# Gate matrix stored by group of experts, and early activations loaded a trip ahead into four buffers

## The chip, the cores and the metric

One core of one Trainium2 chip. The metric is the time of one execution on the device in microseconds (us), the median of several runs. The kernel before ran three times: 4664.34, 4643.26 and 4653.38 us, median 4653.38.

## The reference, cut to what matters

One layer for 640 tokens (8 x 16 of running streams, 512 of a new one), width 2048: a joint projection, two attentions, a gated merge, LayerNorm, and then the expert layer (PEER) which the change touches. Each token picks, for each of 8 heads, 16 of 128 x 128 single-neuron experts, and sums their outputs.

```python
experts = e1 * PEER_KEYS + e2
gate = jax.nn.softmax(sc, axis=-1)
u = jnp.take(u_table, experts, axis=0)
act = jax.nn.gelu(jnp.einsum('nhkd,nd->nhk', u, xt), approximate=False)
w = (gate * act).astype(xt.dtype)
v = jnp.take(v_table, experts, axis=0)
return jnp.einsum('nhk,nhkd->nd', w, v)
```

## The kernel before, in words

**Two ways through the expert layer.** For 256 of the 640 tokens (two blocks of 128) the expert rows are gathered: GpSimd issues an indirect transfer of 128 rows (1 MB) for each of 128 picks, for two tables and two blocks (`gather`, L379), and VectorE takes each of these 512 steps in one pass of 2048 columns (`gather_step`, L1414; L1420 for u rows, L1423 for v rows). Four row buffers rotate. For the other 384 tokens (N2) the layer is dense: all 16384 experts are computed by TensorE, and a gate matrix that is zero for experts not picked selects among them.

**Units.** TensorE's work is cut into units of 1 MB of weights (128 x 2048 f32), streamed by SyncE into two buffers. ScalarE copies a half into the high part (`split_high`, L1021, copy at L1024), GpSimd subtracts for the low part (`low`, L352, L356), and TensorE does three products (high x high, high x low, low x high), 48 matmuls of 384 columns a unit. A group is 4 x 128 experts: four activation units (L639) and four output units (`out_units`, L698, matmul at L703). There are 32 groups. Output units leave partial sums in four PSUM banks, and VectorE adds each into the result (`add_out`, L1436, L1443); a matmul into a bank waits for that add.

**The gate matrix.** Before the late part, a loop of 6 trips (L1001 to L1014) builds it, 64 tokens a trip: VectorE makes one-hot rows (L1403, L1404), TensorE multiplies them (L691) beside the units of the early activations, ScalarE empties the banks into one of two buffers of 2 MB (L1007), and after every 8th of the 96 steps stores one as a block of 32 tokens into the DRAM tensor `gate_matrix` (`G_s`, L134), 16 KB in a row per partition (L1011). `early_activation` (L975) in steps 8 and 15 of each trip stores a 192 KB activation (L980): the activations of the first 4 groups (16 units) are made here, as no gates exist yet. At the end ScalarE waits for the stores (L1018) before it copies the first late weights, and GpSimd does so as well (L441).

**The late part.** Its order is written out. First `EARLY` = 4 trips (L1096) of 12 units: four activation units of group 4+i, its four output units, and four output units of early group i. Then 24 plain groups of 8 units. For each group ScalarE loads that group's gates for all 384 tokens into `G4` (`load_gates`, L1026): per partition 12 pieces (one per block of 32 tokens) of 4 x 32 values, 512 bytes. VectorE multiplies activations by gates (`product`, L1426, L1429), ScalarE copies the high part of the products (`high_part`, L1031, L1033), VectorE makes the low part (`low_part`, L1431, L1433). For an early group the activations come back from DRAM into `act_t` (L190), two buffers, by `load_act` (L1035): the first two are issued behind the trip's first gate load, and the last two when the low parts of the first two are done, both within the trip. VectorE waits for each in `early_product` (L1526).

```python
                for e in range(2):
                    load_act(i, q, e, 8 * i + 2)
                for v in range(2):
                    out_unit(2 * i, first + EG, v, k + EG + v)
                for e in range(2):
                    high_part(q, e, 1, act_t[e])
                out_unit(2 * i, first + EG, 2, k + EG + 2)
                for e in range(2, 4):
                    load_act(i, q, e, 8 * i + 7 + e - 2)
```

**What orders the rest.** The gather steps are dealt over the positions (units) of the late part by a table of room per unit (`ROOM`, `deal`, `STEPS`). GpSimd runs per unit two subtractions and, between them, the gathers dealt to it (`position`, L416); VectorE runs its steps between products and adds; ScalarE's queue holds copies, gelu, the gate loads and the activation loads in program order. All transfers share 16 transfer engines.

## Time and profile before

| | |
|---|---|
| median of 3 runs | 4653.38 us (4643.26 to 4664.34) |
| the profiled execution's own time | 4646.84 us |
| its span | 4645.1 us |
| TensorE matmuls busy | 4319.6 us (93%) |
| VectorE / GpSimd / ScalarE busy | 2683.9 / 2586.4 / 1060.3 us |
| transfers | 1082.02 MB, 233 GB/s over the span |
| gate store / gate load / early activation load, issue to landing (median) | 6.3 / 15.6 / 10.9 us |

The durations of the sections below are from the profiled execution, one run whose own time is 4646.84 us; it lies 6.5 us under the median. "Busy" counts an engine's instructions, not its waits; a transfer share of 1.0 means that all 16 engines had packets under way the whole time (packets of different queues can overlap a little, so the share can pass 1).

### The profile page before, as it was taken

What the parts mean: (1) busy time and instruction counts of PE and PEld (TensorE: products, weight loads), DVE (VectorE), ACT (ScalarE), POOL (GpSimd) and SP (SyncE); (2) the same over time, 40 slices, a digit from 0 to 9 for tenths busy, and PEclk for the clock granted to TensorE, in tenths of its full rate; (3) what the DMA queues carried; (4) which work ended last, traced back from release to release, by engine and by line L of the source; (5) the groups of instructions that cost most, each with busy time, mean ns of one, the idle gap of its engine ahead of it and who ended that gap; (6) DMA issues with size and microseconds to landing.
All of it is one profiled execution on the core that took longest, in us unless ns stands there. A gap on an engine that the chain in (4) does not pass through costs nothing.

```text
span 4645.1 us, 71896 instructions
## 1 busy us (share of the span) xinstructions
PE 4319.6 (93%) x26508; PEld 4144.1 (89%) x26508; DVE 2683.9 (58%) x4808; ACT 1060.3 (23%) x1861; POOL 2586.4 (56%) x1653
## 2 busy tenths in 40 slices
PE   8999999999989997985888999999999999999997
PEld 8999888878889996985878999999999999999996
DVE  1000233344442314898896777777777777777776
ACT  1000122222221102101223222222223222223223
POOL 4455322222235453443335777877777878777783
PEclk9999999999999999997999999999999999999998
DMA  5222322322233221111447999999999999999994
GB/s 199 99 100 95 118 109 102 111 88 78 78 136 121 100 95 54 63 63 56 172 158 287 362 366 366 399 398 402 398 392 377 396 387 406 394 396 400 386 411 199
DMA packets 265977, 1082.02 MB, mean 233 GB/s; under 512 B 24496, under 2 KB 89136, under 8 KB 181168
## 3 DMA queue, kind: packets, MB, share of 16 engines
q0 software_dynamic: 74736, 544.24, 28.7%
q1 hardware_dynamic: 87840, 388.01, 22.6%
q10 hardware_dynamic: 103328, 148.96, 9.4%
q8 instruction: 25, 0.41, 0.0%
q14 instruction: 48, 0.39, 0.0%
HBM read 1019.65 MB, written 66.85 MB: 234 GB/s over the span
## 4 chain that ended last, share of the span: by engine, by line
PE 60%; DVE 12%; POOL 10%; DMA 8%; issue 7%; ACT 1%; ACTq 0%; DVEq 0%; POOLq 0%
PE banks L461 29%; PE banks L703 12%; PE banks L639 11%; POOL w_lo L356 7%; POOL work L384 2%; DMA work<-in_v_rows,idx_all 2%; DMA work<-in_u_rows,idx_all 2%; PE banks L530 2%; PE banks L492 1%; PE banks L691 1%; DMA work<-early_act 1%; DVE work L1404 1%; DMA rows_own<-in_v_rows,idx_all 1%; PE banks L500 1%; DVE mv_hi L1403 1%
## 5 line engine op out<-in xcount | busy, mean ns | idle before, releaser
L356 POOL TENSOR_TENSOR w_lo<-w_raw,w_hi 128x1024 fp32r<-128x1024 f32 x480 | 1154.6, 2406 | 414.2 <-ACT w_hi L1024 409.7
L362 POOL TENSOR_SCALAR w_hi<-w_raw 128x2048 fp32r<-128x2048 f32 x130 | 253.1, 1947 | 1475.7 <-PE banks L461 1269.0
L461 PE MATMUL banks<-mv_hi,w_hi 128*128 128x256 f32 x3648 | 863.5, 318 | 62.1 <-DVE mv_lo L1150 37.5
L461 PE MATMUL banks<-mv_lo,w_hi 128*128 128x256 f32 x3648 | 836.2, 311 | 0.0
L461 PE MATMUL banks<-mv_hi,w_lo 128*128 128x256 f32 x3648 | 835.1, 310 | 0.0
L703 PE MATMUL banks<-mv_hi,w_hi 128*128 128x384 f32 x2048 | 704.2, 344 | 92.9 <-DVE work L1443 82.7
L461 PEld LDWEIGHTS banks<-mv_hi,w_hi 128*128 128x128 f32 x3648 | 652.3, 189 | 125.9 <-issue 102.5
L1024 ACT ACTIVATE w_hi<-w_raw 128x1024 fp32r<-128x1024 f32 x480 | 507.5, 1060 | 998.6 <-PE banks L703 741.8
L639 PE MATMUL banks<-mv_hi,w_hi 128*128 128x384 f32 x2048 | 695.8, 340 | 15.2 <-POOL w_lo L356 11.5
L703 PE MATMUL banks<-mv_hi,w_lo 128*128 128x384 f32 x2048 | 697.2, 340 | 0.0
L703 PE MATMUL banks<-mv_lo,w_hi 128*128 128x384 f32 x2048 | 697.2, 340 | 0.0
L366 POOL TENSOR_TENSOR w_lo<-w_raw,w_hi 128x512 fp32r<-128x512 f32 x520 | 681.9, 1343 | 10.8
L639 PE MATMUL banks<-mv_lo,w_hi 128*128 128x384 f32 x2048 | 687.2, 336 | 0.0
L639 PE MATMUL banks<-mv_hi,w_lo 128*128 128x384 f32 x2048 | 687.0, 335 | 0.0
L461 PEld LDWEIGHTS banks<-mv_lo,w_hi 128*128 128x128 f32 x3648 | 669.7, 189 | 0.0
L461 PEld LDWEIGHTS banks<-mv_hi,w_lo 128*128 128x128 f32 x3648 | 669.1, 189 | 0.0
L1423 DVE SCALAR_TENSOR_TENSOR banks<-work,subkt,banks 128x2048 f32<-128x2048 f32 x192 | 451.6, 2352 | 102.3 <-DMA work<-in_v_rows,idx_all 101.8
L1420 DVE CUSTOM_DVE_ANT_0 work<-work,banks 128x2048 f32<-128x2048 f32 x192 | 438.0, 2283 | 106.0 <-DMA work<-in_u_rows,idx_all 103.7
L703 PEld LDWEIGHTS banks<-mv_hi,w_hi 128*128 128x128 f32 x2048 | 394.7, 193 | 110.7 <-DVE work L1443 94.9
L639 PEld LDWEIGHTS banks<-mv_hi,w_hi 128*128 128x128 f32 x2048 | 387.2, 189 | 16.0 <-issue 11.7
L703 PEld LDWEIGHTS banks<-mv_lo,w_hi 128*128 128x128 f32 x2048 | 394.8, 193 | 0.0
L703 PEld LDWEIGHTS banks<-mv_hi,w_lo 128*128 128x128 f32 x2048 | 394.1, 192 | 0.0
(155 smaller groups left out, 4788.2 us busy)
## 6 DMA issues: line engine op xcount, KB each, us to landing
w_raw<-in_wstream SPq DMA_DIRECT2D x480, 512.0 KB, 7.9
w_raw<-in_wstream SPq DMA_DIRECT2D x130, 1024.0 KB, 4.8
gate_matrix<-work ACTq DMA_DIRECT2D x12, 2048.0 KB, 6.3
work<-gate_matrix ACTq DMA_DIRECT2D x32, 768.0 KB, 15.6
out_p<-work ACTq DMA_DIRECT2D x34, 320.0 KB, 2.2
work<-out_p ACTq DMA_DIRECT2D x34, 320.0 KB, 3.4
gate_scratch<-work ACTq DMA_DIRECT2D x32, 320.0 KB, 2.2
work<-gate_scratch ACTq DMA_DIRECT2D x16, 640.0 KB, 3.9
```

The source lines that it names most:

```text
L356: pool.tensor_tensor(w_lo[s][:, part], raw[s][:, part], w_hi[s][:, part].bitcast(f32), ALU.subtract) \
L362: pool.tensor_scalar(w_hi[s][:, :], raw[s][:, :], 1.0, 0.0, ALU.mult, ALU.add).then_inc(hi_done, 1)
L366: last = pool.tensor_tensor(w_lo[s][:, part], raw[s][:, part], w_hi[s][:, part].bitcast(f32), ALU.subtract)
L384: pool.indirect_dma_start(rows_t[n % ROWS], None, (u_rows, v_rows)[pick // PICKS % 2], bass.IndirectOffsetOnAxis(ap=idx_all[:, pick:pick + ...
L461: last = pe.matmul(acc(dst, h), a[s][:, P * k:P * k + P], b[h][:, k, :], start=(k == k_first and n == 0), stop=(k == k_last and n == 2))
L492: last = pe.matmul(bank[:, 0:w], q_t[rows, end - P:end], k_t[rows, end - w:end], start=True, stop=True)
L530: last = pe.matmul(o, v_nat[:, P * kb + HD * hh:P * kb + HD * hh + HD], pt[:, P * c:P * c + P], start=(c == 0), stop=(c == nk - 1))
L639: last = pe.matmul(banks[:, bank, 0:N2], a[s][:, P * k:P * k + P], b[1][:, k, :], start=(k == 0 and n == 0), stop=(k == KT_N - 1 and n == 2))
L703: last = pe.matmul(banks[:, d, 0:N2], a[v % 2][:, at:at + P], b[z][:, e, :], start=(e == 0 and n == 0), stop=(e == EG - 1 and n == 2))
L1024: act.activation(w_hi[s][:, HALVES[h]], raw[s][:, HALVES[h]], ACT.Copy).then_inc(hi_late, 1)
L1420: ins = dve.tensor_tensor_reduce(rows, rows, nat, 1.0, 0.0, ALU.mult, ALU.add, act_n[:, pick % PICKS:pick % PICKS + 1])
L1423: ins = dve.scalar_tensor_tensor(nat, rows, act_n[:, pick % PICKS:pick % PICKS + 1], nat, ALU.mult, ALU.add)
```

## The change

The DRAM tensor of the gate matrix is laid out as (group, partition, block, expert, token) in place of (block, partition, expert, token). A gate load is then one row of 6 KB per partition; a gate store writes, for each partition, 32 pieces of 512 bytes, one per group. `act_t` has four buffers in place of two (the two new ones lie in columns 2304 to 3071 of the same work area, free in the late part until the last sums), with a semaphore each, and the four activations of an early group are loaded together: for trip 0 right behind the very first gate load, for trip i+1 at the end of trip i's first set of output units, behind the gate load that stands there. In the trip itself nothing is loaded but gates.

```diff
@@ -131,7 +131,7 @@
         bs_a = dram("bias_sample_a", (16, P, 144))
         a_s = dram("early_act", (N_EARLY, P, N2))
         hb_s = dram("block_h", (P, D))
-        G_s = dram("gate_matrix", (GBLK, P, KEYS, GT))
+        G_s = dram("gate_matrix", (GROUPS, P, GBLK, EG, GT))
 
         raw = [sb(f"w_raw{s}", [P, D]) for s in range(2)]
         w_hi = [sb(f"w_hi{s}", [P, D], f32r) for s in range(2)]
@@ -187,7 +187,7 @@
         psum = W2[:, 2688:2688 + N2]
         mean_t, rstd_t = W2[:, 0:T], W2[:, T:2 * T]
         sq_t = x_res
-        act_t = [W2[:, N2 * s:N2 * s + N2] for s in range(2)]
+        act_t = [W2[:, N2 * s:N2 * s + N2] for s in (0, 1, 6, 7)]
         pick_t = [W2[:, N2 * (q + 2):N2 * (q + 3)] for q in range(3)]
         oh1 = W2[:, 5 * N2:5 * N2 + 8 * P].rearrange("p (n e) -> p n e", n=8)
         G4 = W2[:, 2 * N2:6 * N2].rearrange("p (b e t) -> p b e t", b=GBLK, e=EG)
@@ -283,7 +283,7 @@
 
         oh_ready, g_full, g_evac = sem("oh_ready"), sem("g_full"), sem("g_evac")
         act_stored = [sem(f"act_stored{s}") for s in range(2)]
-        act_in = [sem(f"act_in{s}") for s in range(2)]
+        act_in = [sem(f"act_in{e}") for e in range(EG)]
 
         rows_in = [sem(f"rows_in{s}") for s in range(ROWS)]
         idx_ready, acc_high, rows_used, nat_ready, act_n_ready, act_n_gelu = (
@@ -1008,8 +1008,8 @@
                                    banks[:, 2 + q % 2, :].rearrange("p (t e) -> p e t", t=4), ACT.Copy).then_inc(g_evac, 1)
                     if qq == 7:
                         act.wait_ge(g_evac, 16 * i + q + 3)
-                        act.dma_start(G_s[ds(2 * i + w, 1)].rearrange("a p e t -> p (a e t)"),
-                                      g_buf[w].rearrange("p e t -> p (e t)")).then_inc(g_stored[w], 16)
+                        act.dma_start(G_s[:, :, ds(2 * i + w, 1), :, :].rearrange("g p a e t -> p g (a e t)"),
+                                      g_buf[w].rearrange("p (g e) t -> p g (e t)", e=EG)).then_inc(g_stored[w], 16)
                     if q in (8, 15):
                         early_activation(TAIL + 2 * i + q // 15, q // 15, TAIL // 2 + i)
 
@@ -1025,17 +1025,17 @@
 
             def load_gates(g, q):
                 act.wait_ge(w_prod, 1 + 4 * q)
-                act.dma_start(G4.rearrange("p b e t -> p b (e t)"),
-                              G_s[:, :, ds(EG * g, EG), :].rearrange("b p e t -> p b (e t)")).then_inc(g4_in, 16)
+                act.dma_start(G4.rearrange("p b e t -> p (b e t)"),
+                              G_s[g].rearrange("p b e t -> p (b e t)")).then_inc(g4_in, 16)
 
             def high_part(q, e, z, src):
                 act.wait_ge(w_prod, 1 + 4 * q + e + 1)
                 act.activation(ww_hi[z][:, e, :], src, ACT.Copy).then_inc(wwh_done, 1)
 
-            def load_act(g, q, e, after):
-                act.wait_ge(w_ready, after)
-                act.dma_start(act_t[e % 2], a_s[ds(EG * g + e, 1)].rearrange("a p t -> p (a t)")) \
-                    .then_inc(act_in[e % 2], 16)
+            def load_acts(i):
+                act.wait_ge(w_ready, 8 * i + 2)
+                for e in range(EG):
+                    act.dma_start(act_t[e], a_s[EG * i + e]).then_inc(act_in[e], 16)
 
             def act_units(g, q, first):
                 for e in range(EG):
@@ -1093,24 +1093,20 @@
                     split_high(v % 2, (first - U_LATE) // 2 + 1 + v // 2, 1)
 
             load_gates(EARLY, 0)
+            load_acts(0)
             for i in range(EARLY):
                 first, q, k = U_LATE + 12 * i, 2 * i + 1, 12 * i
                 for e in range(EG):
                     act_unit(EARLY + i, 2 * i, first, e, k + e)
                 load_gates(i, q)
-                for e in range(2):
-                    load_act(i, q, e, 8 * i + 2)
-                for v in range(2):
+                for v in range(EG):
+                    if v >= 2:
+                        for e in (2 * v - 4, 2 * v - 3):
+                            high_part(q, e, 1, act_t[e])
                     out_unit(2 * i, first + EG, v, k + EG + v)
-                for e in range(2):
-                    high_part(q, e, 1, act_t[e])
-                out_unit(2 * i, first + EG, 2, k + EG + 2)
-                for e in range(2, 4):
-                    load_act(i, q, e, 8 * i + 7 + e - 2)
-                for e in range(2, 4):
-                    high_part(q, e, 1, act_t[e % 2])
-                out_unit(2 * i, first + EG, 3, k + EG + 3)
                 load_gates(EARLY + i + 1, q + 1)
+                if i + 1 < EARLY:
+                    load_acts(i + 1)
                 for v in range(EG):
                     out_unit(q, first + 2 * EG, v, k + 2 * EG + v)
             for g in range(2 * EARLY, GROUPS):
@@ -1524,8 +1520,8 @@
                         steps(k + e + 1, 1)
 
             def early_product(i, e):
-                dve.wait_ge(act_in[e % 2], 16 * (2 * i + e // 2 + 1))
-                product(act_t[e % 2], e)
+                dve.wait_ge(act_in[e], 16 * i + 16)
+                product(act_t[e], e)
 
             for i in range(EARLY):
                 q, first, k = 2 * i + 1, U_LATE + 12 * i + EG, 12 * i
@@ -1540,7 +1536,7 @@
                             early_product(i, e)
                     if v >= 2:
                         for e in (0, 1) if v == 2 else (2, 3):
-                            low_part(q, e, 1, act_t[e % 2])
+                            low_part(q, e, 1, act_t[e])
                     add_out(2 * i, v, first, parts=range(2))
                     if v > 1:
                         steps(k + EG + v, 1)
```

## Rows read from the trace of the kernel before

**Rows 1.** The page: busy time of each engine, and the transfer share in 40 slices.
```profile
PE 4319.6 (93%) x26508; PEld 4144.1 (89%) x26508; DVE 2683.9 (58%) x4808; ACT 1060.3 (23%) x1861; POOL 2586.4 (56%) x1653
...
DMA  5222322322233221111447999999999999999994
```

**Rows 2.** Windows by stage: length, busy PE, PEld, DVE, ACT, POOL, clock, share, GB/s.
```profile
2240.00:2460.00 220.00, 178.78 (x1218) 171.91 (x1216) 216.90 (x698) 57.68 (x100) 65.03 (x47) 0.97 0.41 160
2460.00:2900.00 440.00, 399.29 (x2203) 395.05 (x2204) 312.56 (x371) 125.61 (x147) 320.50 (x187) 0.95 0.93 354
2900.00:3400.00 500.00, 485.55 (x2749) 482.03 (x2748) 380.66 (x338) 145.44 (x172) 396.38 (x243) 0.99 1.01 399
```

**Rows 3.** Windows: one trip, one group, and behind one stall.
```profile
2544.30:2657.20 112.90, 103.19 (x576) 101.92 (x576) 82.39 (x99) 30.51 (x37) 81.78 (x50) 0.97 0.95 365
...
3734.00:3804.20 70.20, 68.16 (x384) 67.84 (x384) 50.22 (x59) 20.26 (x24) 54.07 (x33) 0.98 0.99 384
...
2545.00:2560.00 15.00, 15.00 (x78) 15.00 (x77) 13.53 (x15) 2.92 (x4) 11.92 (x8) 0.86 0.87 297
```

**Rows 4.** Chain of waits, 3040 to 3110 us.
```profile
3059.07 33.28 PE banks L639 x192
```

**Rows 5.** TensorE's timeline at its stalls; idle time and its releaser in brackets.
```profile
2544.32 0.69 PE L703 MATMUL banks<-mv_hi,w_hi 128*128 128x384 f32 x1 [5.34 <-DVE work L1443]
...
2768.83 0.69 PE L703 MATMUL banks<-mv_hi,w_hi 128*128 128x384 f32 x1 [5.18 <-DVE work L1443]
...
2881.79 0.69 PE L703 MATMUL banks<-mv_hi,w_hi 128*128 128x384 f32 x1 [5.73 <-DVE work L1443]
...
2962.28 0.44 PE L703 MATMUL banks<-mv_hi,w_hi 128*128 128x384 f32 x1 [2.00 <-DVE work L1443]
...
3734.02 0.69 PE L703 MATMUL banks<-mv_hi,w_hi 128*128 128x384 f32 x1 [3.82 <-DVE work L1443]
```

**Rows 6.** VectorE's timeline, 2533 to 2545 us.
```profile
2533.37 0.08 DVE L1420 DVE_READ_ACCUMULATOR2_ANT subkt<- 128x1 f32 x1
2538.76 0.56 DVE L1429 TENSOR_TENSOR work<-work 128x384 f32<-128x384 f32 x1 [5.30 <-DMA work<-early_act]
2542.09 0.56 DVE L1429 TENSOR_TENSOR work<-work 128x384 f32<-128x384 f32 x1 [2.77 <-DMA work<-early_act]
...
2543.72 1.01 DVE L1443 TENSOR_TENSOR work<-work,banks 128x384 f32<-128x384 f32 x2
```

**Rows 7.** ScalarE's timeline, 2504 to 2531 us (ACTq: issues of transfers).
```profile
2504.16 5.51 ACTq L1037 DMA_DIRECT2D work<-early_act  x1
...
2513.57 2.01 ACT L1024 ACTIVATE w_hi<-w_raw 128x1024 fp32r<-128x1024 f32 x2 [7.75 <-issue]
...
2530.70 0.90 ACTq L1037 DMA_DIRECT2D work<-early_act  x2
```

**Rows 8.** Queues (packets, MB, share): rows 3663.3-3734, gate loads 4000-4600, one store 2254-2262.
```profile
q0 software_dynamic: 2576, 18.73, 64.8%
...
q10 hardware_dynamic: 12416, 6.29, 3.7%
...
q10 hardware_dynamic: 128, 2.10, 61.9%
```

**Rows 9.** ScalarE's timeline at the end of the gate matrix.
```profile
2456.99 0.34 ACTq L1011 DMA_DIRECT2D gate_matrix<-work  x1
...
2458.17 0.34 ACTq L980 DMA_DIRECT2D early_act<-work  x1
2464.04 1.06 ACT L1024 ACTIVATE w_hi<-w_raw 128x1024 fp32r<-128x1024 f32 x1 [6.04 <-DMA early_act<-work]
```

**Rows 10.** ScalarE's timeline around a gate store in the build stage.
```profile
2256.63 0.34 ACTq L1011 DMA_DIRECT2D gate_matrix<-work  x1
...
2259.86 0.60 ACT L1007 ACTIVATE work<-banks 128x512 f32<-128x512 f32 x1 [2.21 <-PE banks L691]
2264.63 0.60 ACT L1007 ACTIVATE work<-banks 128x512 f32<-128x512 f32 x1 [4.17 <-PE banks L691]
```

## Prediction

> **What bounds the kernel now.** I read the page's busy shares first: TensorE is busy for 93% of the span, and in the page's slices the share of the transfer engines is 9 from slice 22 on [rows 1]. So the kernel falls into a part where only TensorE is full and a part where the transfers are full as well. The windows by stage say which wait counts where [rows 2]. While the gate matrix is built (2240 to 2460 us) VectorE is busy for 216.9 of 220 us and the transfer engines for 41%: VectorE sets that stage. In the four early trips (2460 to 2900) TensorE is busy for 399 of 440 us and the transfers for 93%. In the plain groups behind them TensorE has 97% and the transfers 1.01, 399 GB/s.
>
> Cut into one trip (12 units) and one group (8 units) the balance is plain [rows 3]: a trip lasts 112.9 us with TensorE busy for 103.2 and a transfer share of 0.95; a group lasts 70.2 us with 68.2 and 0.99. The chain of waits has a stretch with 192 matmuls in 33.28 us, 173.3 ns each [rows 4]. A trip's 576 matmuls would take 99.8 us at that, a group's 384 66.6 us. The rest is what can be won.
>
> TensorE's timeline shows where the rest sits [rows 5]. In each of the four early trips (three of the stalls stand there) TensorE waits 5.2 to 5.7 us for VectorE's add at L1443, always at the same place, and restarts with a 0.69 us matmul. In the 24 plain groups the common stall is about 2 us (3.82 in the longest). Behind the stall at 2544 the granted clock is 0.86 over 15 us [rows 3], a part of them at 1.2 instead of 2.4 GHz: 78 matmuls ran where 15 / 0.1733 = 87 fit, 1.5 us lost.
>
> Why VectorE is late there is in its own timeline [rows 6]: from 2533.4 it waits 5.30 us for an early activation, then 2.77 us for the next, and only at 2543.72 does it come to the adds that TensorE stands for. ScalarE issued these two loads at 2530.70, since their buffers were those of the first two activations; they had landed for it 8.1 and 11.4 us later, behind weights and rows [rows 7]. The same view shows a second thing: the first two loads, issued right behind the gates' 1536 pieces of 512 bytes, hold ScalarE for 5.51 us and then until 2513.57, where its next copy of weights could begin.
>
> **The change part by part.**
> *Four activation buffers.* This removes the 5.30 + 2.77 us from VectorE. Its chain products, high copies, low parts, adds then starts at 2533.4 and needs, as at 2538.8 to 2543.7 without the second wait, about 2.2 us; a copy by ScalarE lies between. The adds come at about 2535.6 to 2536, 3 us before TensorE arrives (2544.32 - 5.34 = 2538.98). So the whole 5.3 us goes, and with it the 1.5 us of slow clock: 112.9 - 6.8 = 106.1 us per trip. What is late next is the transfers: 0.95 x 112.9 = 107.3 us of engine time per trip, less 2 x 0.8 for the gates (below), 105.7 us. Both sides say 106: 7 us per trip, **-28 us** over four. Ends: -32 (8 per trip, transfers at a share just above 1) and -14, if half comes back in another wait.
>
> *Where the loads go now.* Four loads of 192 KB are issued in a row behind the trip's last gate load, a trip ahead; for trip 0 at 2464 in place of nothing. On ScalarE that is four issues of some 0.4 us where the next one is not held. They stand ahead of the next weight copy, which GpSimd's subtraction and then its row gathers wait for. The work that hides the 1.6 us is the other unit's matmuls, 48 x 173 ns = 8.3 us; without that cover it would be up to 6 us over four trips. The load waits for the last low part of its trip, which comes 1.2 us after the product that the gate load waits for. At 2464 TensorE needs its first product only after a unit of matmuls. I cost both at 0.
>
> *Gates read as 6 KB pieces.* A 512-byte piece costs one engine 0.037 x 16 x 600 / 12416 = 28.6 ns, so a gate load holds each engine for 96 x 28.6 = 2.75 us. 6 KB pieces are not in this trace; the nearest are the 8 KB pieces of the rows, 25.5 bytes per ns with the small packets among them (18.73 MB in 0.648 x 16 x 70.7 us), and the 16 KB pieces of the gate store, 0.619 x 16 x 8 / 128 = 619 ns or 26.5 bytes per ns [rows 8]. So 8 x 241 ns = 1.93 us, 0.82 us less per load. 23 loads lie in the plain groups, where the share is 0.99 to 1.01: at most -19 us. The least is 0, if VectorE's latency from row to row and not the engines' time sets the pace. I take two thirds, **-12 us**, as the share is full but the packets' own times stretch when they meet. The early trips' part is in the 106 above, and ScalarE is no longer held for the 5.5 and 3.8 us; only a 2 us stall could hang on that, which I keep for the range.
>
> *Gates written as 512-byte pieces.* 12 stores of 2 MB, each now 256 pieces per engine instead of 8. A store of 512 bytes does not occur before; priced like the load, 256 x 28.6 = 7.3 us against 8 x 619 = 4.95: 2.4 us more. At 26.5 bytes per ns it would be 0 more, at twice the load's price 9.7. The last store is on the path: it is issued at 2456.99, the early activation's store behind it in the same queue at 2458.17, and ScalarE's next copy, which TensorE's first late unit waits for, begins at 2464.04 [rows 9]. **+2.4 us.** The other 11 have 16 steps of 1.9 us or more before their buffer is needed and lie under VectorE.
>
> *What stands behind the long stores.* The early activation's store comes 1.2 us after every second gate store. If it is held as the loads of [rows 7] were, ScalarE stands until most of the 7.3 us are through, some 8.6 us after the issue, and cannot empty the gate banks. Before, the next two copies came 3.2 and 8.0 us after the issue [rows 10]; with two banks VectorE notices a copy late by more than about 3.9 us (two of its 1.94 us steps). So between 0 and 12 x 1.5 = 18 us; most of it fits, **+2 us**.
>
> Sum: -28 - 12 + 2.4 + 2 = -35.6 us. The profiled execution took 4646.84 us (span 4645.1 plus 1.7 around it), which gives 4611; from the median of the runs, 4653.38, it is 4618. The three runs spread over 21 us, so I say 4614.
>
> **A rule beside the rows.** The Trainium skill, "DMA: Bandwidth & Descriptors", section "Latency and other measured facts", says that copies whose rows lie 2 MiB apart in HBM ran at 164 GB/s where others had some 214, and 103 at 4 MiB. The old load has its pieces 2 MB apart, and its row gives 17.9 bytes per ns for 512-byte pieces, which small pieces alone may explain; the new store has them 768 KB apart, which no run here shows. By that rule the store would run a quarter or a half slower, 2 to 8 us more for each store; the sum does not use it.
>
> **The rivals.**
> *Plain groups gain nothing.* For: their common stall is 2 us on VectorE's adds, and a row's way (gather, landing, VectorE, next gather) may set the pace, not the engines' sum. Against: a share of 1.0 in every window. -28 + 4.4: 4623 to 4630. That the load is still cut into 512-byte packets would look the same.
> *A new wait in the trips.* The packets of 6 KB and four activations land as one burst of 1.9 + 2 us per engine, just where VectorE starts the second set of output units; rows come late by up to 4 us and TensorE stands on L1443 again. Half the trips' gain and none in the groups: -14 + 4.4, 4637 to 4643.
> *Everything counts.* -32 - 19 with a cheap store: 4596 to 4602.
> *Slower: scattered 512-byte writes.* Place: the 12 gate stores. At 80 ns a piece a store takes 20.5 us; ScalarE is held about 17 us after the issue, and VectorE loses 17 - 8 to 17 - 3.2 less 3.9, 5 to 10 us at each of 12 places, 90 us, and 15 at the end: 4647 + 105 - 40 = 4712. It decides from about 65 ns a piece. Against: 512-byte reads, scattered over all 24 MB, take 28.6 ns, and the 16 KB writes run at 26.5 bytes per ns. The skill's rule above points this way, though its factor of two gives 57 ns only.
>
> **How the numbers follow.** About 0.5%, 23 us, is what a measurement here can tell: faster is below 4630, slower above 4677. Chances: the forecast 0.50 (4600 to 4628), plain groups gain nothing or uncut pieces 0.23, the new wait 0.15, everything counts 0.08, slower 0.04. Faster takes the first, the fourth and about two thirds of the second, 0.74; same 0.22; slower 0.04. The range leaves out the slow case and the outer ends: 4592 to 4642.
>
> **What the profile after would show.** Right: no stall of 5 us on L1443 in the trips, no wait of VectorE on early_act, a trip of 105 to 107 us with a share near 1; gate loads landing in under 12 us; groups of 69.5 to 70 us; no ScalarE issue over 1 us after 2470. From the last gate store's issue to ScalarE's next copy, 7.1 us before [rows 9], about 9.5. Wrong: the store's packets over 45 ns each, VectorE under 95% in the build stage, ScalarE's early_act store issues of many us, or a new stall on L1443 just behind the burst.

## The result and the profile after

The changed kernel takes **4628.15 us** (median of 9 runs, 4614.49 to 4639.95), the one before 4649.67 us in the runs beside it (9 runs, 4643.26 to 4664.34): ratio **0.9948**, 95% interval 0.9934 to 0.9962. A second set of 6 runs gave 4625.26 us and 0.9943 (0.9924 to 0.9961). So it is faster, by 21.5 and 27.5 us, about the 0.5% that the prediction calls measurable. The forecast was 4614 us in a range of 4592 to 4642. The profiled execution took 4623.17 us (span 4621.4), against 4646.84 before.

From the page of the kernel after, busy time and transfer share; from its transfer view, two issues (KB each, median us from issue to landing).

```profile
PE 4310.1 (93%) x26508; PEld 4132.5 (89%) x26508; DVE 2676.7 (58%) x4808; ACT 1060.7 (23%) x1861; POOL 2581.3 (56%) x1653
...
DMA  5222322222233221111457999999999999999994
...
gate_matrix<-work ACTq DMA_DIRECT2D x12, 2048.0 KB, 9.2
early_act<-work ACTq DMA_DIRECT2D x16, 192.0 KB, 5.5
```

TensorE's busy time fell by 9.5 us of 4320 [rows 1] with the same 26508 matmuls; the rest of the 23.7 us between the spans, 14.2, is idle time. The gate store lands in 9.2 us (6.3 before), the activation stores in 5.5 (2.1 before, by the same view). For the gate load this profile gives no landing; the second profile of the same kernel (experiment 1) gives 9.4 us, where it was 15.6.

The windows of the kernel after, by stage, then three whole trips (columns as in [rows 2]).

```profile
2240.00:2460.00 220.00, 181.89 (x1228) 174.23 (x1226) 216.74 (x698) 56.69 (x98) 68.28 (x50) 0.96 0.54 163
2460.00:2900.00 440.00, 408.03 (x2318) 402.67 (x2317) 324.01 (x391) 132.75 (x154) 334.61 (x197) 0.98 0.96 374
2900.00:3400.00 500.00, 484.35 (x2763) 481.41 (x2762) 382.90 (x332) 146.62 (x174) 397.59 (x244) 0.99 1.00 400
...
2546.80:2653.50 106.70, 101.20 (x577) 99.60 (x576) 80.39 (x99) 30.64 (x36) 81.26 (x50) 1.00 0.98 386
2653.50:2758.90 105.40, 101.06 (x578) 99.71 (x578) 80.50 (x99) 30.67 (x37) 81.39 (x50) 1.00 0.98 391
2758.90:2865.10 106.20, 101.25 (x578) 99.66 (x577) 80.46 (x99) 30.70 (x37) 81.35 (x50) 1.00 0.97 388
```

The gain sits in the second window: 408.0 us of matmuls in 440, where there were 399.3 [rows 2]. A trip lasts 105.4 to 106.7 us, where the one of [rows 3] took 112.9, and its clock is 1.00 instead of 0.97. In the third window nothing is to be seen. The waits of VectorE between 2470 and 2900 us say what went:

```profile
DVE work L1416 <- DMA work<-in_u_rows,idx_all: 51.4, 42, 3.2
DVE banks L1425 <- ACT banks L1080: 25.5, 4, 20.2
DVE work L1439 <- PE banks L703: 18.4, 17, 1.5
```

(Total us, number, longest; L1439 is the add that was L1443, L1425 the product that was L1429, L1416 the u row step.) No wait on an early activation and none on the gates is among them; before, the activations alone cost VectorE 33.5 us here (its waits for u rows were 37.8 us then, 51.4 now). TensorE still waits for that add in the trips, but none of the waits of 5 us is left. Its waits there, kernel before (2468 to 2960 us) and then kernel after (2475 to 2944):

```profile
PE banks L703 <- DVE work L1443: 31.8, 9, 5.7
...
PE banks L703 <- DVE mv_lo L1433: 1.7, 3, 0.7
```

```profile
PE banks L703 <- DVE work L1439: 15.4, 13, 2.4
PE banks L703 <- DVE mv_lo L1429: 5.3, 4, 2.6
```

**Where the 23.7 us between the two profiled spans are**, cut at events that both kernels have (the last one-hot row of VectorE, TensorE's first late matmul, the 10th and the 32nd gate load of ScalarE):

| stretch | before | after | difference |
|---|---|---|---|
| start to the last one-hot row | 2453.8 | 2457.9 | +4.1 |
| from there to the first late matmul | 13.9 | 16.3 | +2.4 |
| on to the 10th gate load (the early trips) | 492.64 | 470.25 | -22.4 |
| on to the 32nd gate load (22 plain groups) | 1542.37 | 1534.79 | -7.6 |
| on to the end | 142.4 | 142.2 | -0.2 |

The windows of the two long stretches, the kernel before and then the one after (length, busy PE and number of matmuls first):

```profile
2467.68:2960.32 492.64, 458.92 (x2544) 454.03 (x2544) 354.81 (x417) 140.23 (x167) 366.78 (x216) 0.96 0.94 362
2960.32:4502.69 1542.37, 1491.79 (x8448) 1480.22 (x8448) 1160.57 (x1076) 450.60 (x534) 1213.72 (x742) 0.99 1.00 396
```

```profile
2474.20:2944.45 470.25, 449.57 (x2546) 444.08 (x2547) 350.61 (x421) 140.98 (x167) 365.77 (x216) 0.99 0.97 381
2944.45:4479.24 1534.79, 1483.97 (x8448) 1472.66 (x8446) 1160.13 (x1072) 450.62 (x534) 1211.27 (x742) 0.99 0.99 397
```

In the trips 13.0 of the 22.4 us are idle time of TensorE (33.7 before, 20.7 after) and 9.3 are busy time: the granted clock is 0.99 where it was 0.96. In the plain groups the idle time did not move (50.6 and 50.8 us). The 7.6 us are busy time (7.8 us less), with the same 8448 matmuls: the granted clock over the stretch is 0.992 where it was 0.988 (the view rounds both to 0.99). Each profile was taken a second time (experiments 1 and 5) and says the same: idle 53.5 us in both kernels, busy 1483.2 after and 1491.6 before.

The 4.1 us are not the change's: the first one-hot row already comes 4.3 us later (2222.6 after, 2218.3 before), and in the other profiles of this study it comes anywhere from 2213.8 to 2224.1.

### The profile page after: what moved, and what is told of

It reads as the page before. It is cut to its first block, busy times and chain, and to the rows that moved or that the text cites. A ratio compares the mean times of both kernels' runs of the same rounds, so it can differ in the third digit from the quotient of the medians.

```text
span 4621.4 us, 71896 instructions
## 1 busy us (share of the span) xinstructions
PE 4310.1 (93%) x26508; PEld 4132.5 (89%) x26508; DVE 2676.7 (58%) x4808; ACT 1060.7 (23%) x1861; POOL 2581.3 (56%) x1653
## 4 chain that ended last, share of the span: by engine, by line
PE 59%; DVE 12%; POOL 11%; DMA 8%; issue 7%; ACT 1%; ACTq 1%; DVEq 0%; POOLq 0%
PE banks L461 29%; PE banks L703 11%; PE banks L639 10%; POOL w_lo L356 8%; DMA work<-in_u_rows,idx_all 3%; POOL work L384 2%; DMA work<-in_v_rows,idx_all 2%; PE banks L530 2%; PE banks L691 2%; PE banks L492 2%; DMA rows_own<-in_u_rows,idx_all 1%; PE banks L500 1%; POOL rows_own L384 1%; DVE work L1312 1%; DMA work<-out_p 1%
## 5 line engine op out<-in xcount | busy, mean ns | idle before, releaser
L639 PE MATMUL banks<-mv_hi,w_hi 128*128 128x384 f32 x2048 | 696.4, 340 | 17.6 <-POOL w_lo L356 13.9
L1416 DVE CUSTOM_DVE_ANT_0 work<-work,banks 128x2048 f32<-128x2048 f32 x192 | 438.3, 2285 | 126.9 <-DMA work<-in_u_rows,idx_all 124.5
```

Of the source, the lines that this page charges most:

```text
L639: last = pe.matmul(banks[:, bank, 0:N2], a[s][:, P * k:P * k + P], b[1][:, k, :], start=(k == 0 and n == 0), stop=(k == KT_N - 1 and n == 2))
L1416: ins = dve.tensor_tensor_reduce(rows, rows, nat, 1.0, 0.0, ALU.mult, ALU.add, act_n[:, pick % PICKS:pick % PICKS + 1])
```

## Experiments

Up to four stretches are told of each profile: the trips (first late matmul to 10th gate load), the plain groups (10th to 32nd gate load) and, where they matter, the time from the last one-hot row to the first late matmul, called the seam, and the one from the first one-hot row to the last, called the build stage (235.5 us before, 235.3 after). Ratios are to the kernel before, run beside it on the same chip, each with its 95% interval.

**1. The changed kernel again**, unedited.

> The changed kernel once more, unchanged, beside the kernel before on this chip: how far the profile's stages repeat. If the three terms read from the first pair of traces are real, the stretch from the first gate load to the first plain group's gate load is again 22 to 24 us shorter than before, the plain groups 5 to 10 us, the tail of the last gate store 2.4 us longer, and the 4.1 us that this profile was later when the build stage began (nothing of the change runs there) comes out anywhere between -5 and +5. If the upstream 4 us belong to the change, they come back as +4. Ratio 0.993 to 0.997.

4625.26 us, 0.9943 (0.9924 to 0.9961). Trips 468.3 us, plain groups 1536.7, seam 17.3, build stage 236.3. The first one-hot row comes at 2216.9 us, earlier than before, so the 4.1 us don't return.

**2. Buffers alone.** The layout of before, with four activation buffers and the loads a trip ahead:

```diff
-        act_t = [W2[:, N2 * s:N2 * s + N2] for s in range(2)]
+        act_t = [W2[:, N2 * s:N2 * s + N2] for s in (0, 1, 6, 7)]
...
+            load_acts(0)
...
+                if i + 1 < EARLY:
+                    load_acts(i + 1)
```

> Four activation buffers and the loads a trip ahead, but the gate matrix laid out by block as before. Theory 1 (the parts add): the trips' gain of 22 to 24 us stays but for 0.8 us per gate load, 15 to 20 us in all, plain groups and the store's tail as before: ratio 0.9955 to 0.9970. Theory 2 (the parts need each other): the four loads now stand behind 1536 pieces of 512 bytes in the same queue, ScalarE is held for 9 us or more at each trip's end, weights and row gathers come late, and TensorE stalls there again: trips of 109 us or more, gain under 12 us, ratio above 0.9974.

Measured: 4673.25 us, **1.0044** (1.0024 to 1.0065), slower than before. The trips take 500.2 us, the plain groups 1542.7. VectorE's waits in the trips (2470 to 2920 us), and two of TensorE's stalls from its timeline:

```profile
DVE work L1416 <- DMA work<-in_u_rows,idx_all: 44.8, 34, 3.0
DVE work L1425 <- DMA work<-gate_matrix: 26.8, 4, 7.1
...
2663.78 0.66 PE L703 MATMUL banks<-mv_hi,w_hi 128*128 128x384 f32 x1 [4.91 <-DVE work L1439]
...
2777.28 0.69 PE L703 MATMUL banks<-mv_hi,w_hi 128*128 128x384 f32 x1 [4.91 <-DVE work L1439]
```

The wait for the activations is gone, as the theory said, and another stands in its place, once a trip: the chain product for the gates themselves. The stall of TensorE is back with nearly its old size (4.91 us against 5.18 to 5.73 in [rows 5]). The other half of Theory 2 did not come: ScalarE is not held, its issues of the activation loads behind the gate load take 0.45 to 1.15 us each. VectorE's timeline shows the wait in place:

```profile
2662.20 1.06 DVE L1425 TENSOR_TENSOR work<-work 128x384 f32<-128x384 f32 x2 [7.08 <-DMA work<-gate_matrix]
2663.18 1.93 DVE L1439 TENSOR_TENSOR work<-work,banks 128x384 f32<-128x384 f32 x4
```

This is not a wait that the one for the activations had covered. In the last three trips VectorE comes to this product some 13.3 us after the issue of the gate load, as it did before; but the gates land 20.3 to 20.4 us after it, where they had landed after 12.8 to 13.2, just in time, and VectorE waited 0.2 to 0.3 us. (The 5.3 and 2.8 us of [rows 6] stood at the later pair of activations.) Why the same 1536 pieces were faster before, the queues and GpSimd's timeline show. In the kernel before, the gate load is issued at 2617.63:

```profile
2618.05 8.11 ACTq L1037 DMA_DIRECT2D work<-early_act  x2
...
2627.41 2.41 POOL L356 TENSOR_TENSOR w_lo<-w_raw,w_hi 128x1024 fp32r<-128x1024 f32 x1 [8.50 <-ACT w_hi L1024]
2629.96 0.95 POOL L384 DMA_INDIRECT work<-in_u_rows,idx_all  x1
```

The two activation loads right behind it held ScalarE for 8.11 us, so that its copies, GpSimd's subtraction and the next row gather came late, 12.3 us after the issue. In this kernel nothing stands behind the gate load, and the next gather comes after 6.2 us. The queues in the 3 us from 9 us after the issue, kernel before (2626.6 to 2629.6) and then this one (2650.8 to 2653.8):

```profile
q10 hardware_dynamic: 1342, 0.84, 102.7%
q0 software_dynamic: 17, 0.07, 6.1%
```

```profile
q10 hardware_dynamic: 634, 0.32, 42.1%
q1 hardware_dynamic: 94, 0.39, 35.2%
q0 software_dynamic: 56, 0.43, 35.1%
```

Before, the gates (q10, with the activations behind them) had the engines almost to themselves. Now rows and weights go on beside them, and short pieces take long in such company; experiment 12 shows at what rate. No run here keeps the hold and takes away the wait, so this reading rests on the two traces.

Not all of the 20 us that this kernel loses is shown to be the edit's. In its profile the trips are 7.6 us longer than before, and the build stage 17.2 us (252.7), at a granted clock of 0.92 instead of 0.97, though the code of that stage is that of the kernel before. Experiment 11 comes back to it.

**3. Layout alone.** Group layout with two activation buffers; the diff is that of the lines on `G_s`, the store and `load_gates` alone.

> The gate matrix by group, but two activation buffers loaded within the trip as before. Theory 1 (the wait for the activations makes the trips' stall, the layout only shortens transfers): VectorE still waits 7 us or so for the last two activations and TensorE 4 to 5.5 us in each trip; trips of 110 to 112 us; plain groups 7 us shorter in sum, tail of the store 2.4 us longer: 5 to 10 us faster in all, ratio 0.9978 to 0.9990. Rival (short pieces were what made the activation loads slow): the loads land in 6 us or less, the stall falls under 2 us and the trips are as in the changed kernel: ratio 0.9955 or less.

Measured: 4649.66 us, **0.9993** (0.9978 to 1.0007). Trips 493.7 us, plain groups 1541.1, seam 17.3. Here VectorE waits for the activations as before, 25.7 us in 11 waits, and never for the gates. So each part alone gains nothing in the trips (500 and 494 us against 493), and both together gain 22 to 24. With two buffers the later pair of activations still comes late; with four and short pieces the gates do; only with four and long pieces does neither.

**4. A later wait.** In the changed kernel ScalarE waits for the stores only ahead of the first gate load, no longer ahead of its weight copies:

```diff
-            for w in range(2):
-                act.wait_ge(g_stored[w], 16 + 16 * (GBLK // 2))
-                act.wait_ge(act_stored[w], 16 * (N_EARLY // 2))
...
+            for w in range(2):
+                act.wait_ge(g_stored[w], 16 + 16 * (GBLK // 2))
+                act.wait_ge(act_stored[w], 16 * (N_EARLY // 2))
             load_gates(EARLY, 0)
```

> The changed kernel with ScalarE's wait for the gate and activation stores moved from ahead of the first four weight copies to just ahead of the first gate load (the copies need neither). If the last store is on the path as read (2461.07 to 2470.57 in the changed kernel), TensorE's first late matmul comes 7 to 9.5 us earlier and the whole is 6 to 9 us faster than the changed kernel. Rival: the first product then waits for gates that arrive later than TensorE's first unit (8.3 us) allows, and 3 us or less remain; or the row transfers are the real bound from there on and nothing remains.

Measured: 4623.73 us, 0.9937 (0.9916 to 0.9958). From the last gate store to the first late matmul it is 9.8 us where the kernel after has 13.1, so 3.3 us are won at that place; the time as a whole (1.5 us under experiment 1) can't tell it. The theory's 7 to 9.5 us did not come there. Seam and trips together are 478.5 us (12.9 and 465.5), against 486.5 after and 485.6 in experiment 1, but the build stage, which the edit does not touch, took 246.1 us in this profile, so whether the whole gains 6 to 9 us stays open.

**5. The kernel before again**, for the spread of a profile.

> The kernel before once more, for its stages: first late matmul to the gate load of the first plain group was 492.6 us, from there to the last gate load 1542.4. In the runs so far the latter was 1534.8 and 1536.7 for the changed kernel, 1541.1 with the layout alone, 1542.7 with the buffers alone. If the short pieces cost the plain groups anything that can be told, this run gives 1540 us or more; if they differ by chance, it gives a value between 1534 and 1540. It also shows whether the build stage (235.5 us from the first one-hot to the last in the first trace, 252.7 with the buffers alone, whose code there is the same) changes from run to run.

4654.3 us, one run; trips 493.7, plain groups 1545.0, against 492.6 and 1542.4 in the first profile. These stretches repeat within 1 to 3 us; the build stage of other kernels does not (234.4 to 252.7 us over all profiles here).

**6. Fewer gate bytes in the plain groups.** There only the gates of block 0, 64 KB, are read. The gates of the other 352 tokens are left as they lie in the buffer, so this kernel's outputs are not the layer's.

```diff
+                if g >= 2 * EARLY:
+                    act.dma_start(G4[:, 0].rearrange("p e t -> p (e t)"),
+                                  G_s[g, :, 0].rearrange("p e t -> p (e t)")).then_inc(g4_in, 16)
+                    return
```

> The changed kernel, but in the 24 plain groups only the gates of the first 32 of the 384 tokens are loaded (64 KB in place of 768 KB; the others use stale gates): 8 packets of 512 bytes per engine, some 0.23 us, in place of 1.93. 24 x 1.7 = 41 us less time of the transfer engines. Theory 1 (the transfer engines' time sets the pace of the plain groups): 30 to 41 us faster than the changed kernel. Theory 2 (VectorE's rows come at a pace set by four buffers, each with a landing of some 9 us, and the gates only brush it): 5 to 15 us faster. Theory 3 (TensorE and the order of VectorE's steps set it): 0 to 4 us.

Measured: 4624.78 us, 0.9947 (0.9928 to 0.9965), no other than the kernel after; plain groups 1532.6 us, trips 466.5. Eleven twelfths of the bytes of 22 loads, some 39 us of engine time by the 1.93 us that the prediction gave a load, bring about 2 us.

**7. Twice the gate bytes.** Each plain group reads 768 KB more, as two transfers of 3 KB pieces into columns that nothing reads.

```diff
+                if g >= 2 * EARLY:
+                    for n, m in enumerate((m1_hi, m1_lo)):
+                        act.wait_ge(act_in[n], 16 * EARLY + 16 * (g - 2 * EARLY))
+                        act.dma_start(m[:, 3072:3840].bitcast(f32),
+                                      G_s[g, :, 6 * n:6 * n + 6].rearrange("p b e t -> p (b e t)")).then_inc(act_in[n], 16)
```

> The changed kernel, but each plain group's gate load is followed by a second reading of the same 768 KB into unused columns, as two loads of 3 KB pieces that nobody waits for: 24 x 2.0 = 48 us more time of the transfer engines. Theory 1 (engines' time): 38 to 48 us slower than the changed kernel. Theory 2 (pace of the row buffers): 8 to 25 us. Theory 3: 0 to 5 us.

Measured: 4631.3 us, 0.9954 (0.9934 to 0.9974); plain groups 1539.7 us, +5. So in the plain groups, where the windows show a transfer share of 1.0, neither 40 us of engine time less nor as much more moves the time by more than 5 us. The engines' time does not set the pace there, and the gain of the longer pieces, if there is one, isn't engine time. TensorE's idle time is 49.1 us in experiment 6 and 52.3 here, 50.8 in the kernel after.

**8. Close pieces of 512 bytes.** By-group layout with 128 bytes of padding behind each 512, so that a load is cut into 1536 pieces again, 640 bytes apart instead of 2 MB. A store still writes 512 bytes at a time, as in the kernel after.

```diff
-        G_s = dram("gate_matrix", (GROUPS, P, GBLK, EG, GT))
+        G_s = dram("gate_matrix", (GROUPS, P, GBLK, EG * GT + 32))
```

> The changed kernel with its layout by group, but 128 bytes of padding behind each block's 512, so that a gate load is again 1536 pieces of 512 bytes, now 640 bytes apart instead of 2 MB apart. Theory 1 (the number of pieces makes the load slow beside rows and weights, since each waits its turn behind larger packets): as with the buffers alone, VectorE waits some 25 us in the four trips for the gates, trips of 112 us or more, ratio 1.000 to 1.005. Rival (the distance of the pieces in memory made it slow, as the Trainium skill's page DMA: Bandwidth & Descriptors has it for rows 2 MiB apart): the gates land in 12 us or less, no wait in the trips, time as the changed kernel, ratio 0.993 to 0.996.

Measured: 4667.89 us, **1.0034** (1.0017 to 1.0051). Trips 509.0 us, plain groups 1544.2. VectorE's waits from 2460 to 2980 us:

```profile
DVE work L1425 <- DMA work<-gate_matrix: 35.0, 4, 14.6
```

That is experiment 2 over again (1.0044): the loads are late with pieces 640 bytes apart as well, so the distance is not what makes them late, and their number is.

**9. The small store ahead of the large one**, on top of experiment 4: at step 15 the early activation's store is issued before the gate store.

```diff
+                    if q == 15:
+                        early_activation(TAIL + 2 * i + 1, 1, TAIL // 2 + i)
                     if qq == 7:
...
-                    if q in (8, 15):
-                        early_activation(TAIL + 2 * i + q // 15, q // 15, TAIL // 2 + i)
+                    if q == 8:
+                        early_activation(TAIL + 2 * i, 0, TAIL // 2 + i)
```

> The changed kernel with ScalarE's wait for the stores moved down to the first gate load (as in the run with the late wait), and in step 15 of each build trip the early activation's store issued ahead of the gate store in place of behind it. In the run with the late wait alone the early activation's store held ScalarE for 4.69 us behind the gate store's pieces, and the first late matmul came 9.8 us after the gate store's issue (13.1 to 14.2 in the changed kernel). Theory (that hold is what is left): no ScalarE issue over 1 us at the end of the build, the first late matmul 4 to 5 us after the gate store's issue, tail and trips together 472 to 476 us in place of 482 to 483, the whole 5 to 10 us faster than the changed kernel: ratio 0.992 to 0.9935. Rival: the first gates now arrive later than VectorE's first product needs them (store 9 us, load 4 us) and the gain falls under 3 us.

Measured: 4621.42 us, 0.9929 (0.9913 to 0.9946). ScalarE's timeline at the seam, of this kernel and then of the kernel after:

```profile
2453.00 0.35 ACTq L980 DMA_DIRECT2D early_act<-work  x1
2453.53 0.39 ACTq L1013 DMA_DIRECT2D gate_matrix<-work  x1
2454.16 3.89 ACT L1023 ACTIVATE w_hi<-w_raw 128x1024 fp32r<-128x1024 f32 x4 [1.32 <-issue]
```

```profile
2461.07 0.39 ACTq L1011 DMA_DIRECT2D gate_matrix<-work  x1
...
2462.29 4.70 ACTq L980 DMA_DIRECT2D early_act<-work  x1
2470.57 1.06 ACT L1024 ACTIVATE w_hi<-w_raw 128x1024 fp32r<-128x1024 f32 x1 [8.44 <-DMA early_act<-work]
```

The issue of a small transfer right behind the 2 MB store holds ScalarE for 4.70 us; ahead of it, 0.35. The seam is 8.3 us here, 16.3 after and 13.9 before. About half of that comes back: the trips take 474.0 us, so that both together are 482.3, against 486.5 after, 485.6 in experiment 1 and 478.5 in experiment 4, on which this one builds; the plain groups are unchanged (1534.5). The theory had the hold right, and its 5 to 10 us are not shown: the whole is 3.8 us under experiment 1 and 6.7 under the kernel after, in sets whose runs spread over 8 to 25 us.

**10. One row step first.** The plain groups kept a stall of about 2 us in TensorE, at the first output unit. There VectorE takes all row steps dealt to the unit ahead of the first two adds, in the other three units one. On top of experiment 9:

```diff
-                    steps(k + EG + v, 0, 1 if v else None)
+                    steps(k + EG + v, 0, 1)
                     add_out(g, v, first, g == GROUPS - 1, range(2))
-                    if v:
-                        steps(k + EG + v, 1)
+                    steps(k + EG + v, 1)
```

> The run with the changed store order, and in the 24 plain groups VectorE takes only one row step, not all, ahead of the first two adds of the first output unit; the others come between the second and third add, as in the other output units. Theory (the 2 us stall of TensorE at that place in nearly every plain group is made by the order of VectorE's steps, since neither cutting nor doubling the gate loads moved it by more than 4 us in sum): the stall falls under 0.5 us in most groups and the plain groups take 1500 to 1525 us in place of 1535: 10 to 30 us less. Rival: VectorE as a whole is behind on rows there, the stall moves to the third and fourth bank or the next unit, and the plain groups stay at 1530 or more.

Measured: **4560.55 us** (4559.56 to 4562.2), **0.9798** (0.9781 to 0.9814), 61 us under experiment 9 and the fastest of all. The plain groups take 1483.8 us instead of 1534.5: 67.4 us a group, where 384 matmuls need 66.6. Of these 51 us, 38 are idle time of TensorE (49.0 to 11.2 us) and 13 busy time (granted clock 0.992 to 0.998). The profiles show 51 of the 61 us; the profiled run of experiment 9 was the fastest of its six. TensorE's waits from 3000 to 4400 us, kernel after and then this one:

```profile
PE banks L703 <- DVE work L1439: 39.3, 19, 5.0
PE banks L703 <- DVE mv_lo L1429: 11.4, 14, 1.5
```

```profile
PE banks L703 <- DVE mv_lo L1431: 8.9, 9, 2.2
PE banks L703 <- DVE work L1441: 1.3, 3, 0.6
```

And one of its windows:

```profile
2900.00:3400.00 500.00, 497.41 (x2863) 495.68 (x2862) 395.24 (x340) 153.39 (x184) 412.74 (x253) 1.00 1.01 414
```

The transfers moved 414 GB/s where the kernel after moved 400 at a share of 1.00: the share had been no ceiling.

**11. Buffers alone, again** (the kernel of experiment 2).

> The buffers alone, old layout, for one more trace. If the longer build stage of its first trace (252.7 us, all others with that code 234.5 to 239.4 but one of 246.1) belongs to chance, this one shows 234 to 240 with probability about 3 in 4, and the trips again 498 to 503 us with some 25 us of VectorE waiting for gate_matrix. If the build stage is again above 250, something of this kernel sets it.

4679.61 us, one run. Trips 510.7 us; VectorE waits for the gates 38.1 us, 4 times, the longest 14.3. The build stage takes 242.2 us, outside the 234 to 240 that were given three chances in four, and short of the 250 that would have laid it to this kernel. So the gates are late here again, and the trips lose 18 us where they lost 8 in experiment 2, the build stage 7 where it lost 17. The loss of experiment 2 holds; the trips' share in it is 8 us by one profile and 18 by the other, and why the build stage varies (its granted clock is 0.94 here) is open.

**12. One row step first, in the kernel before.** The edit of experiment 10 alone, with 512-byte gate pieces and two buffers.

> The kernel before, with one edit: in the plain groups VectorE takes only one row step ahead of the first two adds of every output unit (before: for the unit with v = 0 all its steps). Gate layout and activation buffers stay as before. Theory A: the stall of about 2 us in each plain group hangs on this order alone, whatever the gate pieces are; with 512-byte pieces the groups gain what they gained with 6 KB pieces, 51 us (the stretch from the 10th to the 32nd gate load went from 1534.5 to 1483.8 us), so the stretch goes from 1542 to 1489-1494 us and the time to 4590-4604 us, ratio 0.987 to 0.990. Theory B: the transfers are the next limit, and short pieces, 0.8 us of engine time per gate load more, take their part once the stall is gone: the stretch stays above 1505 us and the ratio is 0.991 or more. The trips stay at 493 us in both.

Measured: 4680.38 us, **1.0054** (1.0029 to 1.0079). Both theories fall, Theory A altogether and Theory B by its mechanism: the plain groups take 1567.1 us, 25 more than before (19 of them idle time of TensorE, 6 busy time), with the same edit that took 51 away beside 6 KB pieces. The windows show the transfers less full than before (a share of 0.98 and 391 GB/s from 3400 to 4500 us, where it was 1.00 and 394), not more, and TensorE's and VectorE's waits from 3000 to 4400 us show what stands in place of the stall:

```profile
3400.00:4500.00 1100.00, 1054.37 (x5963) 1045.22 (x5963) 815.84 (x785) 314.17 (x374) 856.55 (x524) 0.98 0.98 391
```

```profile
PE banks L703 <- DVE mv_lo L1433: 55.8, 25, 4.5
...
PE banks L703 <- DVE work L1443: 3.0, 3, 1.6
...
DVE banks L1429 <- DMA work<-gate_matrix: 117.0, 13, 12.5
```

The stall on the add is gone (3.0 us left), so the order did what it did in experiment 10. But now VectorE waits for the gates, 117 us in all, where the kernel before never does in these groups. The median landing of their loads is 38.9 us (21 loads from 3000 to 4500 us), 16.8 in the kernel before. The queues show how a load of 768 KB can take so long. These are the transfers of one load, issued at 3259.80, for whose landing VectorE begins its product only at 3305.69, after 9.29 us of waiting: the queues (packets, MB, share) from 3259.8 to 3265.8 us, then to 3271.8. q0 carries the rows, q1 the weights, q10 the gates.

```profile
q0 software_dynamic: 189, 1.29, 52.1%
q1 hardware_dynamic: 161, 0.59, 26.7%
q10 hardware_dynamic: 852, 0.44, 26.7%
...
q0 software_dynamic: 210, 1.59, 64.7%
q1 hardware_dynamic: 206, 0.77, 32.2%
q10 hardware_dynamic: 209, 0.11, 6.0%
```

In the second stretch each queue sent the same number of packets, 206 to 210, though those of the rows are 8 KB and the gates' 512 bytes. It is no chance of one load: of the load issued at 3115.89, the 6 us from 3127.9 have 217, 222 and 217, and the next 6 have 211, 206 and 212. So while all three queues are full, each gets as many packets as the others. The first stretch does not show this, 852 against 189 and 161; most engines must have had less in the other queues then, which is inferred, as the trace does not tell one engine from another. A turn lasts 16 x 6 / 209 = 0.46 us, and a gate load has 96 pieces on each engine; if all of them met full queues it would take 96 x 0.46 = 44 us. This load landed in 45.9 us, and the latest of all in 47.1. More than half of its pieces had gone in the first 6 us, so most engines were quicker; the slowest one decides. An estimate with the same turn for a load of 8 pieces of 6 KB: one such piece takes 0.24 us instead of 0.03, so 8 x (0.46 + 0.21) = 5.4 us. The kernel after, a load issued at 3286.74, q10 in the 6 us behind it and in the next 6:

```profile
q10 hardware_dynamic: 118, 0.67, 27.0%
...
q10 hardware_dynamic: 26, 0.12, 4.7%
```

128 pieces of 6 KB are a load, 0.79 MB; 0.67 MB went within 6 us, and the 0.12 MB left in the next, with 16 packets of 4 bytes. Over the 22 loads from 2944 to 4479 us the last piece was through 5.9 to 8.9 us after the issue.

## Why the prediction was right, and where not

The direction, the range and the place of most of the gain were right; what the buffers do alone, and what pays in the plain groups, were not. Its 35.6 us came out as 21.5 (27.5 in the second set; 27.8 in the profiled pair without the 4.1 us at the start), short in both terms that win.

**Trips, -28 forecast, -22.4 measured** (-24.3 in experiment 1). The stall of 5 us and the activation waits went, and three whole trips became 6.1, 6.3 and 6.8 us shorter, where 7 was forecast. Their parts are others than forecast. The prediction had 5.3 us of waiting and 1.5 of slow clock for each trip, 21.2 and 6.0 in all; measured are 13.0 of waiting and 9.3 of clock. Its 1.5 us came from the 15 us behind one stall, although in [rows 3] a trip's 103.2 us of matmuls stand 3.4 above the 99.8 at full clock; in the three whole trips the busy time fell by 1.9, 3.3 and 3.6 us. And the trips were taken as four alike: up to the gate load between the first trip's two sets of output units 2.6 us were won, the three whole trips between those loads gave 19.2, and the last 80 us only 0.6, as TensorE now waits 2.6 us there for VectorE's low parts.

**What the term was put down to, was wrong.** The prediction ascribed all 5.3 us to the activation buffers ("So the whole 5.3 us goes") and 1.6 us of transfer time a trip to the layout. Experiments 2 and 3 give each part nothing in the trips. The step that failed is the hold of ScalarE behind the trips' gate load: the prediction saw it ("ScalarE is no longer held for the 5.5 and 3.8 us") and counted its end as a gain or nothing. With it gone the row gathers come 6 us sooner, beside the gates' pieces, and 512-byte pieces then land 7 us later than before, too late for their product (experiment 2). In the change as a whole the 6 KB pieces make this harmless, and so the sum of the term held. The rival "a new wait in the trips" expected a new wait, but from the burst of 6 KB pieces; the new wait belongs to the 512-byte pieces, and the 6 KB pieces are what keeps it away.

**Plain groups, -12 forecast, -7.6 measured** (-5.7 and -6.8 in experiments 1 and 4). The forecast took two thirds of 0.82 us of engine time for each load, since the transfer share was 1.0. Experiments 6 and 7 show that engine time is worth about a tenth there: 7 us between the two, for some 80 us of it. The rival "plain groups gain nothing" had the cause right, the order of VectorE's row steps, and experiment 10 shows it: 51 us went with the stall. The 6 to 8 us gained are no waiting at all: TensorE's idle time stayed at 50.6 and 50.8 us, its waits for the add from 3000 to 4400 us at 40.2 and 39.3, and the matmuls took 7.8 us less at a higher granted clock (0.992 after 0.988). The clock fell to 1.2 GHz eleven times in these groups before and six times after, each time at a stall of TensorE of 1.8 to 5.0 us, but other stalls of 2 us passed without a fall. Why there are fewer in the kernel after is open; layout alone won 1.3 us. That the term came within a factor of two is chance, as nothing that it priced was seen to pay.

**The last store, +2.4 forecast, +2.4 measured** (the seam went from 13.9 to 16.3 us, and to 17.3 in experiments 1 and 3). From the gate store to ScalarE's next copy it is 9.5 us after 7.1 [rows 9], as forecast. The store's pieces take what the load's take: in the 6 us of full queue behind a store the kernel after moves 290 GB/s, 512 x 16 / 290 = 28 ns a piece. With this the slower rival falls, which needed 65 ns. The Trainium skill, "DMA: Bandwidth & Descriptors", section "Latency and other measured facts", has copies whose rows, one of 16 KiB per partition, lie 2 MiB apart at three quarters of the rate. No run here shows that case: the store's pieces are 512 bytes, 768 KB apart, for which the page gives no rate, so the prediction's "By that rule the store would run a quarter or a half slower" went beyond the page. For the load, pieces 2 MB and 640 bytes apart gave 1.0044 and 1.0034 (experiments 2 and 8), with intervals that overlap.

**The hold in the build stage, +2 forecast, 0 measured** (235.5 us before, 235.3 after). The hold itself came: the issue of the small store behind the gate store takes 4.56 us around 2262, and the next bank is emptied 6.3 us after the gate store, where it had been 3.2 [rows 10]. VectorE stayed at 216.7 us busy of 220, since a bank late by less than two of its steps costs nothing. The prediction had that allowance and took 2 us of 18 for its failure; the 18 count twelve places, though by its own words the small store stands right behind every second gate store, six in all.

**Not thought of at all**: how the engines choose between queues. Pieces were costed as engine time, 28.6 ns each, when beside full queues what they cost is a turn each. Experiment 12 shows it in counts of packets. The rule stands in the Trainium skill, "DMA: Bandwidth & Descriptors", section "Queues, rings and completion order": an engine serves its queues in turn and drains a whole packet, which there means some 9 to 17 descriptors, before it switches. The trace agrees in kind, as each queue gets the same share of packets (206, 210 and 209 in 6 us); how many of them an engine sends in one go can't be told from these counts. What stays open is why the tighter order of experiment 12 keeps the other queues full for so much longer than in the kernel before: that gates wait less where other engines stand still was seen twice (experiments 2 and 12), and no run takes it apart.

## What to carry to other kernels

Cost a transfer beside full queues by its number of pieces times a turn of the other queues, not by its bytes, as an upper bound: 96 short pieces on each engine took up to 47 us, 8 long ones some 6 to 9, and whatever held the other queues back meanwhile had been helping the short pieces: experiment 2 took away such a hold, experiment 12 a stall. A transfer share of 1.0 says that the engines always have something to do, not that they are the bound; cut or double one stream and look. Split a stretch's gain into idle and busy time before you name a cause: with the same number of matmuls, less busy time is clock. And test the parts of a change alone: here the buffers gave +0.4%, the layout -0.1%, both -0.5%, and a third edit, the order of VectorE's row steps, was worth -1.3% beside long pieces and +0.5% beside short ones.

## What the runs showed of the hardware that was not expected

- With the three queues full, each sends as many packets as the others whatever their size (210 of up to 8 KB, 206 of up to 4 KB, 209 of 512 bytes in 6 us). The gate loads of experiment 12 landed in 5.0 to 47.1 us, median 33.3.
- Writing 512-byte pieces costs what reading them does, some 28 ns each on one engine, so a 2 MB store lands in 9.2 us against 6.3 with 16 KB pieces.
- Where rows and weights leave the engines alone, 512-byte pieces go fast: 1342 packets of the gates' queue in 3 us, against 634 beside rows and weights (experiment 2). ScalarE's hold behind the load had made that room.
- ScalarE's issue of a small transfer right behind a store of 256 pieces an engine is held 4.6 to 4.7 us; issued ahead of it, 0.35 us.
- The transfers reached 414 GB/s at a share of 1.01 (experiment 10), where 399 had gone with the same share [rows 2].
- The same 8448 matmuls took 1491.8 us of busy time before and 1484.0 after with as much idle time (50.6 and 50.8 us), at a granted clock of 0.988 and 0.992.
